# Two chained transformer blocks on one core: the modulation product half a quarter sooner in the first MLP, its column sums as rows in four groups of 32 output partitions, then turned

## Chip, cores and metric

One Trainium2 chip, one NeuronCore. The metric is device time in microseconds of one execution, the median of several runs. All inputs and outputs are float32.

## What is computed

A 512-token sequence of width 1024 goes through a first block (mixer of convolution and retention, then a squared-ReLU MLP, then a norm) and a second block (adaptive norm, two kinds of attention, squared-ReLU MLP). What matters here is the first MLP and the modulation vector that the second block needs:

```python
def sq_relu_mlp(u, w_up, w_down):
    hdn = jax.nn.relu(u @ w_up)          # w_up 1024 x 4096
    return (hdn * hdn) @ w_down          # w_down 4096 x 1024
...
ada = (c @ w_ada + b_ada)                # c 1 x 1024, w_ada 1024 x 6144
shift1, scale1, gate1, shift2, scale2, gate2 = jnp.split(ada, 6, axis=-1)
h = rmsnorm(x, g_norm1) * (1.0 + scale1) + shift1
```

## The kernel before, in words

Activations lie feature-major: `xres[P, KC, T]` holds 8 chunks of 128 features by 512 tokens. Every large product is made of **units**: one 1024x128 weight block against all 8 chunks of the input, giving 128 output features by 512 tokens in one PSUM bank. Float32 precision comes from three reduced-precision products per chunk, high x high, high x low, low x high, so a unit is 24 matmuls of 512 columns (`unit`, L539 to L555). `two_units` runs two units alternately, chunk by chunk.

The weights of a unit pass through four slots (slot s = unit number mod 4): SyncE issues the load into `raw` (L338) once GpSimd has freed the slot, ScalarE casts it to the high half `w_hi` (L1045), GpSimd subtracts for the low half `w_lo` (L511), TensorE then uses both. ScalarE casts two units ahead (`ahead`), in its program order just before it reads the result of the current unit.

The first MLP goes through four quarters q. A quarter is 8 up units (hidden features) and 8 down units. In this document U0 to U7 are the up units and D0 to D7 the down units of a quarter, of the first quarter where nothing else is said; O0 to O7 are the units of the output projection before it. U0 and U1, and U4 and U5, are run as pairs by `two_units`; the others singly. After each up unit ScalarE makes the ReLU (L1238) and its square, rounded (L1240), VectorE the exact square (L1830) and the low half (L1835); after each down unit VectorE scales (L1852) and adds to `xres` (L1856). D0's and D4's chunks wait for the low halves one by one (`mlp_h`).

The modulation product c @ w_ada is made on VectorE beside this. `w_ada` (24 MB) comes in 32 **pieces** of 128 rows by 1536 columns, 768 KB each, into two buffers `adaw[:, b, :]`. `ada_piece` (L1793 to L1805) multiplies a piece by 128 entries of c and adds it to `acc[128, 6144]`. Pieces stand at every odd unit, U1, U3, U5, U7, D1, D3, D5, D7, with b = 0, 1, 0, 1, and so on; the load of a piece (L420) stands on SyncE's queue right behind the weight load of that unit and waits for `ada_used`, that is for VectorE to be done with the piece that had the same buffer. SyncE, ScalarE, GpSimd, VectorE and TensorE all run their own instructions strictly in the order written here by hand.

What is left is the sum of `acc` over its 128 partitions. TensorE makes it as 48 products `ada_columns` (L777): 128 columns of `acc` as weights, one column of ones as input, one column of output. In the last down units (`with_columns`) a group of two columns follows each of chunks 2 to 7 of D4, D5 and D7; the last twelve come after `both_sums` (the sums for the next norm) and `roots_turned` (its roots, turned into rows). `modulation(0)` (L1807) reads the first half and makes the gains before D7's result, `modulation(1)` the second half after the norm.

Of the kernel before, what the change touches and what calls it, by code (L numbers as in the profile page):

```python
# [27 lines left out]
ALU = mybir.AluOpType  # L28
# [54 lines left out]
MLPS = ["mlp", "mlp2"]  # L83

# [85 lines left out]
def build(nc, tab, x, norm1_g, w_in, conv_w, conv_norm_g, ret_norm_g, w_out, norm2_g, w_up, w_down,  # L170
# [29 lines left out]
    with ctx:  # L200
# [67 lines left out]
        gones = sb("gones", [P, 2], where=one)  # L268
# [60 lines left out]
        def _(sp):  # L329
# [66 lines left out]
            with sp.Fori(0, KC // 4) as i:  # L396
                for s in range(4):
                    load(st_out, s, i, (whole, cols(w_out, i * 4 * P + s * P)))

            def mlp(st, up, down, with_ada):  # L400
                with sp.Fori(0, NF) as q:
                    for d in range(2):
                        with sp.Fori(0, 2) as i:
                            for s in range(4):
                                if d == 0:
                                    src = cols(up, q * D + i * 4 * P + s * P)
                                else:
                                    src = down.rearrange("(q k p) n -> q p k n", q=NF, p=P)[
                                        ds(q, 1), :, :, ds(i * 4 * P + s * P, P)
                                    ].rearrange("q p k n -> p (q k) n")  # L410
                                load(st, s, q * 4 + 2 * d + i, (whole, src))
                                if with_ada and s % 2:
                                    b = s // 2


                                    sp.wait_ge(sem(f"ada_used{b}"), q * 4 + 2 * d + i + 1)
                                    sp.wait_ge(sem("mix_done"), 1)
                                    src = w_ada_2.rearrange("(q k p) n -> q k p n", q=NF, p=P)[
                                        ds(q, 1), d, :, ds(i * 3 * D + b * 3 * D // 2, 3 * D // 2)]
                                    sp.dma_start(adaw[:, b, :], src.rearrange("q p n -> p (q n)")  # L420
                                                 ).then_inc(sem(f"ada_in{b}"), 16)

            mlp(st_mlp, w_up, w_down, True)
# [8 lines left out]
            sp.wait_ge(sem("ada_sum"), 2)  # L432
# [29 lines left out]
            sp.wait_ge(sem("ada_ready"), 2)  # L462
# [74 lines left out]
        def _(pe):  # L537
# [83 lines left out]
            def bias_rows_made():  # L621

                pe.wait_ge(sem("bias_in"), 32)
                pe.matmul(ps[0:HEADS, SB, :], rbias[:], oneh[:, 0:T], start=True, stop=True)
                pe.matmul(ps[0:HEADS, OU, 0:P], rbias[:], oneh[:, T:NREL], start=True, stop=True
                          ).then_inc(sem("brow_done"), 1)

                pe.wait_ge(sem("vrow_in"), 16 * (len(VECS) - 1))
                pe.transpose(ps[:, OU, P:P + NVEC], vrow[:], ident[0:NVEC, 0:NVEC]).then_inc(sem("vec_turned"), 1)
# [145 lines left out]
            def ada_columns(m0, m1, done=False):  # L775
                for m in range(m0, m1):
                    last = pe.matmul(ps[:, (SB, OU)[m // (3 * KC)], m:m + 1], acc[:, m * P:(m + 1) * P], ones[:, 0:1],  # L777
                                     start=True, stop=True)
                if done:
                    last.then_inc(sem("ada_sum"), 1)  # L780

            def with_columns(s, m0, done):


                pe.wait_ge(sem("acc_done"), 2 * (NF * 4 - 1) + m0 // 12)
                for k in range(KC):
                    unit(st_mlp, s, NF * 4 - 1, y_hi, y_lo, part=(k, k + 1), opens=(k == 0), closes=(k == KC - 1))
                    if k >= 2:
                        ada_columns(m0 + 2 * (k - 2), m0 + 2 * (k - 1), done and k == KC - 1)
# [15 lines left out]
            pe.wait_ge(sem("ada_ready"), 2)  # L805
# [231 lines left out]
        def _(act):  # L1037
# [33 lines left out]

            def norm(name, shift):
                if name == "n3":
# [3 lines left out]
                    act.activation(rinv[:, NT:2 * NT], mneg[:, NT:2 * NT], ACT.Sqrt).then_inc(sem("norm_root"), 1)  # L1077
                else:
# [61 lines left out]
            act.wait_ge(sem("vec_turned"), 1)  # L1140
# [87 lines left out]
            def mlp(st, name, next_norm):  # L1228
# [18 lines left out]
                def down(q, i, last=False):  # L1247
                    for s in range(4):
                        if not (last and st is st_mlp2 and s + AHEAD >= 4):
                            ahead(st, s, q * 4 + 2 + i)  # L1250
                        if last is not False and st is st_mlp:
                            m = i * 4 + s
                            square(next_norm, m, "mlp_x", mlp_before(name) + (NF - 1) * KC)
# [275 lines left out]
        def _(dve):  # L1529
# [246 lines left out]

            def wout(st, scale, done, next_norm, gained=False):
                clear_total(next_norm)
                for i in range(KC // 4):
                    for s in range(4):  # L1780
# [7 lines left out]
                        if i * 4 + s < KC - 1:  # L1788
                            add_square(next_norm, i * 4 + s)

            wout(st_out, lambda m: 1.0, "x_mixed", "n2", gained=True)


            def ada_piece(q, d, i, b):
                n = q * 4 + 2 * d + i
                dve.wait_ge(sem(f"ada_in{b}"), 16 * (n + 1))
                dve.wait_ge(sem("acc_done"), 2 * n + b + 1)
                a = acc[:, ds(i * 3 * D + b * 3 * D // 2, 3 * D // 2)]
                c = vec[:, ds(VAT["c_2"] + 2 * q + d, 1)]
                if isinstance(q, int) and q == 0 and d == 0:  # L1800
                    dve.tensor_scalar(a, adaw[:, b, :], c, None, ALU.mult).then_inc(sem("acc_done"), 1)
                else:
                    dve.scalar_tensor_tensor(a, adaw[:, b, :], c, a, ALU.mult, ALU.add).then_inc(sem("acc_done"), 1)  # L1803
                dve.wait_ge(sem("acc_done"), 2 * n + b + 2)
                dve.sem_inc(sem(f"ada_used{b}"), 1)  # L1805

            def modulation(half):  # L1807

                a, c = half * 3 * KC, slice(half * 3 * KC, (half + 1) * 3 * KC)
                gain, g_at = (gain1, VAT["g_norm1_2"]) if half == 0 else (gain2, VAT["g_norm2_2"])  # L1810
                dve.wait_ge(sem("ada_sum"), half + 1)
                dve.tensor_tensor(ada[:, c], ps[:, (SB, OU)[half], c], vec[:, VAT["b_ada_2"] + a:VAT["b_ada_2"] + a + 3 * KC],
                                  ALU.add).then_inc(sem("ada_ready"), 1)
                dve.wait_ge(sem("ada_ready"), half + 1)
                dve.scalar_tensor_tensor(gain[:], ada[:, a + KC:a + 2 * KC], 1.0, vec[:, g_at:g_at + KC],
# [6 lines left out]
            def mlp(st, name, scale, with_ada, next_norm, factor=None):  # L1822
                def up(q):
                    with dve.Fori(0, 2) as i:
                        for s in range(4):
                            if factor is not None and s == 0:
                                wait(dve, sem("mlp_x"), q * KC + mlp_before(name))

                            dve.wait_ge(bank_free[s], st.turn(s, q * 4 + i) + 1)
                            dve.tensor_tensor(nt[:, s % 2, :], nsq[:, s % 2, :], nsq[:, s % 2, :], ALU.mult  # L1830
                                              ).then_inc(sem("mlp_sq"), 1)
                            dve.wait_ge(sem("mlp_sq"), q * KC + i * 4 + (mlp_before(name) + s + 1))
                            dve.wait_ge(sem("mlp_hi"), q * KC + i * 4 + (mlp_before(name) + s + 1))
                            m = ds(i * 4 + s, 1)
                            dve.tensor_tensor(y_lo[:, m, :], nt[:, s % 2:s % 2 + 1, :], y_hi[:, m, :], ALU.subtract  # L1835
                                              ).then_inc(sem("mlp_h"), 1)
                            dve.wait_ge(sem("mlp_h"), q * KC + i * 4 + (mlp_before(name) + s + 1))
                            if with_ada and s % 2:
                                ada_piece(q, 0, i, s // 2)

                def down(q, i, last=False):
                    for s in range(4):
                        final = with_ada and last and i == 1 and s == 3
                        if with_ada and s % 2 and not final:
                            ada_piece(q, 1, i, s // 2)
                        n, m = q * KC + i * 4 + (mlp_before(name) + s), i * 4 + s
                        if factor is None:
                            add(st, q * 4 + 2 + i, s, n, m, scale(m), "mlp_x")
                        else:
                            dve.wait_ge(used[s], st.turn(s, q * 4 + 2 + i) + 1)  # L1850
                            wait(dve, sem("mlp_x"), n)
                            dve.tensor_tensor(nt[:, 0, :], ps[:, s, :], factor[:], ALU.mult  # L1852
# [373 lines left out]
```

## Time and profile before

| | us |
|---|---|
| median of 3 runs | 1390.85 (1390.78 to 1392.7) |
| the profiled execution's own time | 1392.73 |
| its span, first to last instruction | 1390.9 |
| TensorE busy | 1364.6 (98%) |
| VectorE / ScalarE / GpSimd busy | 818.7 / 517.0 / 561.8 |
| mean granted clock of TensorE, share of full speed | 0.994 |
| output projection O3 to O7, and first MLP | about 221 to 609 |
| sums, roots and columns, to the next projection's first matmul | 609 to 618 |

The profile gives for each engine its instructions with start and length. Line numbers are those of the kernel before. "Idle before <-X" names the instruction whose signal ended the engine's wait. Lengths of matmuls overlap: of a stream of them the distance between starts is what counts.

### The profile page before, as it was taken

Reading aid. Unit: us, or ns where it says so; the run is one execution under the profiler, and the core shown is the slowest. Engines: PE = TensorE matmul, PEld = TensorE weight load, DVE = VectorE, ACT = ScalarE, POOL = GpSimd, SP = SyncE. Lnnn points to the kernel's source line nnn. Section 1 sums busy time; section 2 is a strip of 40 time slices with the busy share of each in tenths; the row PEclk is TensorE's granted clock in tenths of the full one; section 3 lists DMA queues with packets and bytes.
Section 4 is the critical chain, followed back from the end, with each engine's and each line's share of the span. In section 5 each row is a group of like instructions: output and inputs, shape, how many; then the busy total and the mean of one; then the engine's idle time right before and its main releaser. Section 6 shows DMA issues by size and latency. Waiting matters only on the chain.

```text
span 1390.9 us, 18371 instructions
## 1 busy us (share of the span) xinstructions
PE 1364.6 (98%) x6358; PEld 1104.4 (79%) x6358; DVE 818.7 (59%) x1074; ACT 517.0 (37%) x794; POOL 561.8 (40%) x230
## 2 busy tenths in 40 slices
PE   7999999999999999999999999999999999999997
PEld 6777787888888888887777777888878888888886
DVE  4455577574765746885988866334554343352474
ACT  4333224331422314234356665322345323142233
POOL 3334245353553545424322223443525535345361
PEclk9999999999999999989999999999999999999999
DMA  7643234366383763623522232333422423323221
GB/s 206 143 84 91 77 106 140 86 191 173 111 236 96 219 184 106 197 55 106 77 73 60 82 92 79 104 91 92 138 74 91 132 80 108 89 88 118 81 91 61
DMA packets 216323, 156.66 MB, mean 113 GB/s; under 512 B 8996, under 2 KB 197792, under 8 KB 216136
## 3 DMA queue, kind: packets, MB, share of 16 engines
q1 hardware_dynamic: 215800, 154.62, 39.8%
q10 hardware_dynamic: 464, 1.27, 0.3%
q8 instruction: 36, 0.59, 0.2%
q14 instruction: 23, 0.19, 0.0%
HBM read 151.13 MB, written 4.74 MB: 112 GB/s over the span
## 4 chain that ended last, share of the span: by engine, by line
PE 50%; DVE 2%; ACT 1%; issue 0%; POOL 0%; ACTq 0%; DVEq 0%
PE ps L551 28%; PE ps L998 12%; PE ps L947 3%; PE ps L886 2%; PE ps L863 1%; PE ps L850 1%; PE ps L836 1%; PE ps L837 1%; DVE work L2069 1%; DVE work L2066 0%; PE ps L840 0%; DVE work L2051 0%; DVE top L2049 0%; DVE sel L2054 0%; POOL w_lo L511 0%
## 5 line engine op out<-in xcount | busy, mean ns | idle before, releaser
L511 POOL TENSOR_TENSOR w_lo<-raw,w_hi 128x1024 fp32r<-128x1024 f32 x222 | 558.4, 2524 | 795.1 <-ACT w_hi L1045 790.3
L551 PE MATMUL ps<-u_hi,w_hi 128*128 128x512 f32 x1016 | 411.4, 405 | 6.8 <-POOL w_lo L511 2.3
L551 PE MATMUL ps<-u_hi,w_lo 128*128 128x512 f32 x1016 | 398.5, 392 | 0.0
L551 PE MATMUL ps<-u_lo,w_hi 128*128 128x512 f32 x1016 | 398.3, 392 | 0.0
L1045 ACT ACTIVATE w_hi<-raw 128x1024 fp32r<-128x1024 f32 x221 | 231.3, 1053 | 247.8 <-PE ps L998 91.0
L551 PEld LDWEIGHTS ps<-u_hi,w_hi 128*128 128x128 f32 x1016 | 193.3, 190 | 48.9 <-issue 5.4
L551 PEld LDWEIGHTS ps<-u_hi,w_lo 128*128 128x128 f32 x1016 | 192.1, 189 | 41.2
L551 PEld LDWEIGHTS ps<-u_lo,w_hi 128*128 128x128 f32 x1016 | 192.8, 190 | 39.2 <-issue 1.9
L551 PE MATMUL ps<-y_hi,w_hi 128*128 128x512 f32 x320 | 126.7, 396 | 0.1
L551 PE MATMUL ps<-y_lo,w_hi 128*128 128x512 f32 x320 | 124.6, 389 | 0.0
L551 PE MATMUL ps<-y_hi,w_lo 128*128 128x512 f32 x320 | 124.6, 389 | 0.0
L1238 ACT ACTIVATE nsq<-ps 128x512 f32<-128x512 f32 x64 | 38.0, 593 | 214.4 <-PE ps L551 214.3
L998 PE MATMUL ps<-w_hi,y_hi 128*128 128x512 f32 x256 | 99.6, 389 | 0.0
L998 PE MATMUL ps<-w_lo,y_hi 128*128 128x512 f32 x256 | 99.6, 389 | 0.0
L998 PE MATMUL ps<-w_hi,y_lo 128*128 128x512 f32 x256 | 99.6, 389 | 0.0
L1830 DVE TENSOR_TENSOR nt<-nsq 128x512 f32<-128x512 f32 x32 | 46.3, 1446 | 62.9 <-ACT nsq L1238 60.9
L1901 DVE TENSOR_TENSOR nt<-nsq 128x512 f32<-128x512 f32 x32 | 38.6, 1207 | 75.1 <-ACT nsq L1238 74.1
L1803 DVE SCALAR_TENSOR_TENSOR acc<-adaw,vec,acc 128x1536 f32 (+1 forms) x28 | 73.8, 2637 | 4.3 <-DVE y_lo L1835 4.0
L551 PEld LDWEIGHTS ps<-y_hi,w_hi 128*128 128x128 f32 x320 | 60.1, 188 | 12.9 <-issue 0.6
L551 PEld LDWEIGHTS ps<-y_hi,w_lo 128*128 128x128 f32 x320 | 60.1, 188 | 12.7
L1923 DVE SCALAR_TENSOR_TENSOR nt<-ps,rinv,gate_row 128x512 f32<-128x512 f32 x21 | 15.8, 751 | 91.6 <-PE ps L998 91.6
L551 PEld LDWEIGHTS ps<-y_lo,w_hi 128*128 128x128 f32 x320 | 60.1, 188 | 12.0 <-issue 0.2
(268 smaller groups left out, 1771.9 us busy)
## 6 DMA issues: line engine op xcount, KB each, us to landing
raw<-w_in SPq DMA_DIRECT2D x69, 512.0 KB, 3.8
raw<-w_mlp SPq DMA_DIRECT2D x64, 512.0 KB, 3.8
adaw<-w_ada SPq DMA_DIRECT2D x32, 768.0 KB, 4.6
raw<-w_up SPq DMA_DIRECT2D x32, 512.0 KB, 6.2
raw<-w_down SPq DMA_DIRECT2D x32, 512.0 KB, 6.5
raw<-w_out SPq DMA_DIRECT2D x16, 512.0 KB, 4.0
bias_rows<-fbrow SPq DMA_DIRECT2D x4, 640.0 KB
xtok<-x SPq DMA_DIRECT2D x4, 512.0 KB, 6.4
```

The source lines that it names most:

```text
L511: pool.tensor_tensor(w_lo[:, s, :], raw[:, s, :], w_hi[:, s, :], ALU.subtract).then_inc(lo_ready[s], 1)
L551: last = pe.matmul(ps[0:cols, bank, :], w[:, s, c], r[:, k, :], start=(k == ks[0] and w is w_hi and r is r_hi), stop=(k == ks[-1] and w is ...
L836: pe.matmul(ps[:, bank, 0:keys], q_up[:, at, q], k_both[:, at, 0:keys], start=True, stop=False)
L886: last = pe.matmul(ps[:, i, :], u[:, k, t], w[:, s, c], start=(k == 0 and u is u_hi and w is w_hi), stop=(k == KC - 1 and u is u_lo))
L947: last = pe.matmul(ps[:, b, :], w[:, 2, c], r[:, k, :], start=(k == k0 and w is w_hi and r is y_hi), stop=(k == k0 + NQ - 1 and w is w_lo))
L998: last = pe.matmul(ps[:, i, :], h[:, k, t], w[:, s, c], start=(k == 0 and h is y_hi and w is w_hi), stop=(k == KC - 1 and h is y_lo))
L1045: act.activation(w_hi[:, s, :], raw[:, s, :], ACT.Copy).then_inc(hi_ready[s], 1)
L1238: act.activation(nsq[:, s % 2, :], ps[:, s, :], ACT.Relu).then_inc(bank_free[s], 1)
L1803: dve.scalar_tensor_tensor(a, adaw[:, b, :], c, a, ALU.mult, ALU.add).then_inc(sem("acc_done"), 1)
L1830: dve.tensor_tensor(nt[:, s % 2, :], nsq[:, s % 2, :], nsq[:, s % 2, :], ALU.mult).then_inc(sem("mlp_sq"), 1)
L1901: dve.tensor_tensor(nt[:, s % 2, :], nsq[:, s % 2, :], nsq[:, s % 2, :], ALU.mult).then_inc(sem("mlp_sq"), 1)
L1923: dve.scalar_tensor_tensor(gated[i], ps[:, i, :], facts[:, i:i + 1], gate_row[:, c], ALU.mult, ALU.mult).then_inc(bank_free[i], 1)
```

## The change

Three things. (1) The order of the pieces: the first two move to O4 and O6 in the output projection, six to U1, U2, U3, U5, U6, U7 of the first quarter, and from D1 on each piece stands half a quarter sooner than before; the last quarter's down half has none. The wait for `mix_done` moves from each piece to one place ahead of O5's load. (2) The sum over partitions: for each 512 columns of `acc` one product with 32 columns of `pick` as weights (one column of ones, the rest zeros), written to output partitions 32g to 32g + 31 of one bank, g = 0 to 3. Four such products (`ada_rows(0, 0)`) go ahead of D4, eight between `both_sums` and `roots_turned`. (3) ScalarE copies that bank to SBUF (`ada_row_copy`), TensorE turns it in four blocks (`ada_turned`), between D5 and D6 and behind `roots_turned`, and `modulation` reads the turned layout.

```diff
+FIRST_PIECES = [(0, 1, 0), (0, 1, 1), (1, 0, 0), (1, 0, 1), (1, 1, 0), (1, 1, 1)]
+PIECES = 8 * NF
...
+            def ada_load(q, d, i, b):
+                sp.wait_ge(sem(f"ada_used{b}"), q * 4 + 2 * d + i + 1)
...
+                sp.dma_start(adaw[:, b, :], src.rearrange("q p n -> p (q n)")).then_inc(sem(f"ada_in{b}"), 16)
+            for i in range(KC // 4):
                 for s in range(4):
                     load(st_out, s, i, (whole, cols(w_out, i * 4 * P + s * P)))
+                    if i == 1 and s == 0:
+                        sp.wait_ge(sem("mix_done"), 1)
+                    if i == 1 and s % 2 == 0:
+                        ada_load(0, 0, 0, s // 2)
...
+            def down_loads(q, with_ada):
+                with sp.Fori(0, 2) as i:
+                    for s in range(4):
+                        down_load(q, i, s)
+                        if with_ada and s % 2:
+                            ada_load(q + 1, 0, i, s // 2)
+
+            for i in range(2):
+                for s in range(4):
+                    up_load(0, i, s)
+                    if s > 0:
+                        ada_load(0, *FIRST_PIECES[3 * i + s - 1])
+            down_loads(0, True)
...
-            def ada_columns(m0, m1, done=False):
-                for m in range(m0, m1):
-                    last = pe.matmul(ps[:, (SB, OU)[m // (3 * KC)], m:m + 1], acc[:, m * P:(m + 1) * P], ones[:, 0:1],
-                                     start=True, stop=True)
+            def ada_rows(n, at, opens=True, closes=True):
+                for g in range(4):
+                    j = 4 * n + g
+                    last = pe.matmul(ps[32 * g:32 * g + 32, SB, :], pick[:, 32 - at:64 - at], acc[:, j * QW:(j + 1) * QW],
+                                     start=opens, stop=closes)
...
-            with_columns(0, 0, False)
-            with_columns(1, 12, True)
-            unit(st_mlp, 2, NF * 4 - 1, y_hi, y_lo)
-            with_columns(3, 24, False)
+            def ada_turned(half):
+                pe.wait_ge(sem("arow_ready"), half + 1)
+                for b in range(4):
+                    last = pe.transpose(ps[:, OU, b * P:(b + 1) * P], adaw[:, half, b * P:(b + 1) * P], ident)
+                last.then_inc(sem("ada_sum"), 1)
+
+            pe.wait_ge(sem("acc_done"), PIECES + 1)
+            pe.wait_ge(sem("squares"), 7)
+            ada_rows(0, 0)
+            for s in range(2):
+                unit(st_mlp, s, NF * 4 - 1, y_hi, y_lo)
+            ada_turned(0)
+            for s in range(2, 4):
+                unit(st_mlp, s, NF * 4 - 1, y_hi, y_lo)
 
             both_sums()
-            pe.wait_ge(sem("acc_done"), 2 * NF * 4 + 1)
-            ada_columns(36, 42)
+            ada_rows(1, 0, closes=False)
+            ada_rows(2, 1, opens=False)
             roots_turned()
-            ada_columns(42, 48, True)
+            pe.wait_ge(sem("ada_ready"), 1)
+            ada_turned(1)
...
+            def ada_row_copy(half):
+                act.wait_ge(sem("ada_sum"), 2 * half + 1)
+                act.activation(adaw[:, half, 0:QW], ps[:, SB, :], ACT.Copy).then_inc(sem("arow_ready"), 1)
...
+                        if gained and i == 1 and s % 2 == 0:
+                            ada_piece(0, 0, 0, s // 2)
...
+                for i in range(2):
+                    for s in range(4):
+                        up_step(0, i, s)
+                        if s > 0:
+                            ada_piece(0, *FIRST_PIECES[3 * i + s - 1])
```

## Rows read from the trace of the kernel before

**Rows 1.** The profile page, busy time by engine.
```profile
PE 1364.6 (98%) x6358; PEld 1104.4 (79%) x6358; DVE 818.7 (59%) x1074; ACT 517.0 (37%) x794; POOL 561.8 (40%) x230
```

**Rows 2.** The waits by releaser, TensorE, 261 to 612 us: total, times, longest.
```profile
PE ps L551 <- POOL w_lo L511: 1.4, 3, 0.5
```

**Rows 3.** The waits by releaser, SyncE's DMA queue, 195 to 620 us.
```profile
SPq L420 <- DVEq L1805: 275.9, 30, 23.9
```

**Rows 4.** The timeline of SyncE's queue, 195 to 345 us: start, length, instruction, count.
```profile
241.42 3.13 SPq L338 DMA_DIRECT2D raw<-w_up  x2
268.83 0.35 SPq L420 DMA_DIRECT2D adaw<-w_ada  x1
269.41 1.00 SPq L338 DMA_DIRECT2D raw<-w_up  x2
```

**Rows 5.** The timeline of ScalarE, 205 to 345 us, idle time and its releaser in brackets.
```profile
272.39 0.60 ACT L1238 ACTIVATE nsq<-ps 128x512 f32<-128x512 f32 x1 [3.06 <-PE ps L551]
...
275.39 1.06 ACT L1045 ACTIVATE w_hi<-raw 128x1024 fp32r<-128x1024 f32 x1 [1.64 <-DMA raw<-w_up]
...
294.15 0.60 ACT L1238 ACTIVATE nsq<-ps 128x512 f32<-128x512 f32 x1 [3.07 <-PE ps L551]
...
299.02 1.06 ACT L1045 ACTIVATE w_hi<-raw 128x1024 fp32r<-128x1024 f32 x1 [3.51 <-DMA raw<-w_down]
...
300.93 1.06 ACT L1045 ACTIVATE w_hi<-raw 128x1024 fp32r<-128x1024 f32 x1 [0.84 <-DMA raw<-w_down]
```

**Rows 6.** The timeline of VectorE, 205 to 345 us.
```profile
217.96 0.69 DVE L1748 TENSOR_TENSOR y_lo<-nt,y_hi 128x512 fp32r<-128x512 f32 x1 [0.70 <-ACT y_hi L1194]
...
262.14 2.19 DVE L1830 TENSOR_TENSOR nt<-nsq 128x512 f32<-128x512 f32 x1 [0.87 <-ACT nsq L1238]
...
264.50 2.63 DVE L1835 TENSOR_TENSOR y_lo<-nt,y_hi 128x512 f32 x1 [0.17 <-DVE nt L1830]
...
267.50 1.02 DVE L1801 TENSOR_SCALAR acc<-adaw,vec 128x1536 f32 x1 [0.38 <-DVE y_lo L1835]
...
291.04 1.02 DVE L1801 TENSOR_SCALAR acc<-adaw,vec 128x1536 f32 x1 [0.37 <-DVE y_lo L1835]
```

**Rows 7.** The timeline of GpSimd, 195 to 345 us.
```profile
261.37 5.21 POOL L511 TENSOR_TENSOR w_lo<-raw,w_hi 128x1024 fp32r<-128x1024 f32 x2 [6.07 <-ACT w_hi L1045]
...
276.52 2.39 POOL L511 TENSOR_TENSOR w_lo<-raw,w_hi 128x1024 fp32r<-128x1024 f32 x1 [4.74 <-ACT w_hi L1045]
```

**Rows 8.** The timeline of TensorE's weight loads in D7, 596 to 609.5 us.
```profile
603.13 0.64 PEld L777 LDWEIGHTS ps<-ones,acc 128*128 128x128 f32 x4
...
604.27 0.64 PEld L777 LDWEIGHTS ps<-ones,acc 128*128 128x128 f32 x4
```

**Rows 9.** The timeline of TensorE, 255 to 262.5 us: a plain float32 product, 512 columns.
```profile
260.32 1.02 PE L565 MATMUL ps<-nsq,ones 128*128 128x512 f32 x2
```

**Rows 10.** The timeline of TensorE, 733 to 745 us: 64 output partitions each.
```profile
734.06 0.27 PE L863 MATMUL ps<-probt_even,vtoks 128*64 128x128 f32 x1
734.07 0.27 PE L863 MATMUL ps<-probt_odd,vtoks 128*64 128x128 f32 x1
734.17 0.27 PE L863 MATMUL ps<-probt_even,vtoks 128*64 128x128 f32 x1
```

**Rows 11.** The timeline of all engines, 600 to 650 us, from D6's end on.
```profile
606.66 2.13 DVE L1815 SCALAR_TENSOR_TENSOR gain<-ada,vec 128x8 f32<-128x8 f32 x1
...
609.31 0.69 DVE L1852 TENSOR_TENSOR nt<-ps,nrs 128x512 f32<-128x512 f32 x1 [0.32 <-PE ps L551]
...
612.52 1.73 PE L777 MATMUL ps<-ones,acc 128*128 128x1 f32 x12
...
616.85 0.75 DVE L1575 SCALAR_TENSOR_TENSOR u_lo<-nt,ada,u_hi 128x512 fp32r<-128x512 f32 x1
...
618.27 0.77 PE L551 MATMUL ps<-u_hi,w_hi 128*128 128x512 f32 x1
```

**Rows 12.** Busy time by stretch: length, PE, PEld, DVE, ACT, POOL, granted clock, DMA.
```profile
620.00:622.00 2.00, 2.00 (x6) 1.52 (x6) 2.00 (x4) 1.07 (x2) 0.00 (x0) 0.50 0.94 340
```

More of the change, by code:

```diff
@@ L267, in build @@
         adaw = sb("adaw", [P, 2, 6 * D // 4], where=one)
-        gones = sb("gones", [P, 2], where=one)
+        gones, pick = sb("gones", [P, 2], where=one), sb("pick", [P, 64], where=one)
         one.close()
@@ L397, in _ @@
                 for s in range(4):
                     load(st_out, s, i, (whole, cols(w_out, i * 4 * P + s * P)))
[L400 to L421, printed above, removed]
@@ L425, in _, with quarter @@
+            def quarter(q, with_ada):
+                with sp.Fori(0, 2) as i:
+                    for s in range(4):
+                        up_load(q, i, s)
+                        if s % 2:
+                            ada_load(q, 1, i, s // 2)
+                down_loads(q, with_ada)
+            with sp.Fori(1, NF - 1) as q:
+                quarter(q, True)
+            quarter(NF - 1, False)
             load(st_idx, 0, 0, (whole, cols(w_in_2, W2_QI)))
@@ L1814, in modulation @@
-                dve.wait_ge(sem("ada_ready"), half + 1)
-                dve.scalar_tensor_tensor(gain[:], ada[:, a + KC:a + 2 * KC], 1.0, vec[:, g_at:g_at + KC],
+                dve.wait_ge(sem("ada_sum"), 2 * half + 2)
+                turned_ada = ps[:, OU, :].rearrange("p (b g r) -> p g b r", b=4, g=4)
+                for n in range(1 + half):
+                    c = slice(a + 16 * n, a + 16 * (n + 1))
+                    dve.tensor_tensor(ada[:, c].rearrange("p (g b) -> p g b", g=4), turned_ada[:, :, :, n],
+                                      vec[:, VAT["b_ada_2"]:VAT["b_ada_2"] + 6 * KC][:, c].rearrange("p (g b) -> p g b", g=4),
+                                      ALU.add).then_inc(sem("ada_ready"), 1)
@@ L1816, in modulation @@
+                dve.wait_ge(sem("ada_ready"), 1 + 2 * half)
+                at = KC + half * 3 * KC
+                dve.scalar_tensor_tensor(gain[:], ada[:, at:at + KC], 1.0, vec[:, g_at:g_at + KC],
                                          ALU.add, ALU.mult).then_inc(sem("gains"), 1)
@@ L1825, in up @@
                         for s in range(4):
[L1826 to L1839, printed above, removed]
+                            up_step(q, i, s)
@@ L1862, in down @@
-                        if last and i * 4 + s < KC - 1:
-                            add_square(next_norm, i * 4 + s)
-                        if with_ada and last and i == 1 and s == 2:
-                            modulation(0)
-                        if final:
-                            ada_piece(q, 1, i, s // 2)
-                if factor is None:
-                    first = 0
-                else:
-                    first = 1
-                    up(0)
-                    dve.wait_ge(sem("norm_sum"), NORMS.index({"mlp": "n2", "mlp2": "n4"}[name]))
-                    dve.tensor_scalar(factor[:], ps[:, SA, :], 1.0 / D, EPS, ALU.mult, ALU.add
-                                      ).then_inc(sem("mean_sq"), 1)
-                    dve.wait_ge(sem("mean_sq"), MLPS.index(name) + 1)
-                    dve.reciprocal(factor[:], factor[:]).then_inc(sem("factor"), 1)
-                    dve.wait_ge(sem("factor"), MLPS.index(name) + 1)
-                    for i in range(2):
-                        down(0, i)
@@ L1883, in mlp @@
-                with dve.Fori(first, NF - 1) as q:
+                        dve.wait_ge(used[s], st.turn(s, q * 4 + 2 + i) + 1)
+                        wait(dve, sem("mlp_x"), n)
+                        dve.tensor_tensor(nt[:, 0, :], ps[:, s, :], factor[:], ALU.mult
+                                          ).then_inc(bank_free[s], 1)
+                        dve.wait_ge(bank_free[s], st.turn(s, q * 4 + 2 + i) + 1)
+                        dve.tensor_tensor(xres[:, ds(m, 1), :], nt[:, 0:1, :], xres[:, ds(m, 1), :], ALU.add
+                                          ).then_inc(sem("mlp_x"), 1)
@@ new lines, in down @@
+                        if last and m < KC - 1:
+                            add_square(next_norm, m)
+                        if last and m == KC - 2:
+                            modulation(0)
+                for i in range(2):
+                    for s in range(4):
+                        up_step(0, i, s)
+                        if s > 0:
+                            ada_piece(0, *FIRST_PIECES[3 * i + s - 1])
+                dve.wait_ge(sem("norm_sum"), NORMS.index("n2"))
+                dve.tensor_scalar(factor[:], ps[:, SA, :], 1.0 / D, EPS, ALU.mult, ALU.add
+                                  ).then_inc(sem("mean_sq"), 1)
@@ L1884, in mlp @@
+                dve.wait_ge(sem("mean_sq"), MLPS.index(name) + 1)
+                dve.reciprocal(factor[:], factor[:]).then_inc(sem("factor"), 1)
+                dve.wait_ge(sem("factor"), MLPS.index(name) + 1)
+                for i in range(2):
+                    down(0, i)
+                with dve.Fori(1, NF - 1) as q:
                     up(q)
```

102 lines of the change are left out of this document (51 added, 51 removed).

## The prediction

> **What bounds the kernel now.** I read the page first: TensorE is busy for 1364.6 of 1390.9 us [rows 1], so only what makes TensorE wait or work counts. Next the waits by releaser, over the first MLP: TensorE waits for split weights three times, 1.4 us in all [rows 2]. There is no slack left to win there, only some to lose. Then the waits of SyncE's DMA queue: from 195 to 620 us it stands for 275.9 us at the modulation load (L420), until VectorE has used up the piece before in that buffer [rows 3]. The queue is strictly in order, so every weight load written behind a modulation load leaves no sooner than that piece is used. Today this harms nothing, because the two buffers alternate every second unit and each is reused after four units. The timelines of the first quarter show by how much: the weights of U4 and U5 are issued at 241.4 us, 31 us before TensorE wants them, and the queue then stands until VectorE's U1 piece ends (267.50 + 1.02 = 268.5) [rows 4, 6].
>
> **Part 1: two pieces in the out projection.** VectorE gets two steps of 1.0 us [rows 6] and SyncE waits for mix_done (VectorE's last conv step ends at 218.65, same group) before it issues the load that follows O4's. The cover is that O5 to O7 are two and more units of 5.44 us ahead, while load, cast and split take 10 us after mix_done; TensorE stands at O2 then. If that cover were gone each load would cost up to 4 us. The loads of U2 and U3 now wait for the pieces of O4 and O6, some 13 us later than before, yet still reach ScalarE as it wants them. I cost this at nothing.
>
> **Part 2: six pieces in eight units.** In U0 to U7 the pieces stand at U1, U2, U3, U5, U6, U7, buffers 0, 1, 0, 1, 0, 1. So U3's load waits for U1's piece, and U4's weights stand behind it; U7's load waits for U5's piece, and D0's weights stand behind that. The distance of four units has become two. With rows of before:
> (a) U1's piece ends at 268.5 today, because its subtraction is held to 267.1 by GpSimd's pair of splits (261.4 to 266.6) [rows 6, 7]. The second of those, U4's, will not be there yet, so I take 267.1. Issue of the modulation load and the weights behind it takes 0.9 us [rows 4]: 268.0. Such a load landed 6.0 us after issue (269.41 to 275.39) [rows 4, 5]: 274.0. Cast 1.06, split 2.4 [rows 5, 7]: 277.5. U4 is due when U3 ends, 272.3 [rows 5]. U4 and U5 alternate chunk by chunk, so after one chunk of 0.68 us TensorE needs U5's weights too. The second load lands 1.9 us after the first (299.02, 300.93) [rows 5], ScalarE puts U2's ReLU and square between the casts, and GpSimd and VectorE take turns: 280.4 against 273.0. **Loss 7.4.**
> (b) U2's ReLU now waits behind the late cast (275.1), its two VectorE steps are each held by a split, its piece ends at 282.3. U6's weights leave at 282.9 and are ready 9.5 us later, 292.4; U5 ends 280.4 + 15 x 0.68 = 290.6. **Loss 1.8.**
> (c) From U5's end (272.3 + 10.9 = 283.2) to its piece's end (292.06) it took 8.9 us [rows 6]; the piece becomes a multiply-add, 0.8 us longer. 290.6 + 9.7 = 300.3, D0's weights leave at 301.2 and are ready at 310.7. U7 ends at 292.4 + 10.9 = 303.3. **Loss 7.4.**
> (d) U6's ReLU stands behind D0's cast on ScalarE (308.3). VectorE then has four steps and U6's piece, three of them held by the splits of D0 and D1; U7's low half comes at 318.0, while D0's last chunk is due at 315.5. **Loss 2.5.**
> (e) D2's weights wait for U6's piece (316.1) and are ready at 326.2; D1 ends at 324.2. **Loss 2.0.** Behind D3 the distance is four units again.
> Sum 21.1. Below, if GpSimd never held VectorE (each step 0.69), the same working gives 4.7 + 5.3 + 1.0 = 11. Above, each of the two long stops brings TensorE's clock down: the next paragraphs price it. I take 21, because the held steps stand in the rows.
>
> **Part 3: the last down half.** Removed: 36 single-column products in D4, D5 and D7, in groups of two. With a group between them, chunks start 1.14 us apart (603.13, 604.27) [rows 8] instead of 0.68, so 0.46 a group: 6 groups a unit, 5.5 in D4 and D5, 2.8 in D7. U4 to U7 took 294.15 - 272.39 = 21.76, or 5.44 a unit [rows 5]. Added before D4: four float32 products of 512 columns. One such product, two instructions, spans 1.02 us with its drain [rows 9], 0.86 in a row (an estimate from that and the 0.17 of drain). Two products with 64 output partitions start 0.01 apart and the pair repeats every 0.11 [rows 10], so two run side by side. I take four side by side for 32 partitions, 0.9 and 0.3 for changing shape; one after another it would be 3.4. ScalarE's copy lies beside D4; four turns of 128 columns are 0.5. Net for D4 to D6: 5.5 - 1.7 = 3.8.
> The Trainium skill, TensorE: Matmul & The Clock Gate, Part 3, states a speedup of 2.38 for three such column tiles. No row here has four; by that figure the twelve products would take some 4.3 us and not 2.6, and the sum would be 1.7 higher.
> D7 gives back less than its 2.8, since VectorE is late next: between D6's result and D7's it makes the sums and the first gains, of which one step is held for 2.13 us by a split [rows 11]. Today D7's long unit hides that (VectorE even waits 0.32 us, to 609.31 [rows 11]). Without the columns I have VectorE ready 6.4 us after D6's end and TensorE after 5.4: gain 2.8 - 1.0 = 1.8.
>
> **Part 4: between D7 and the index projection.** The eight row products (1.7 us) replace twelve columns (1.73) [rows 11] ahead of the roots' turn: even. The other twelve go from behind it. TensorE began the next unit at 618.27, though its first input was ready at 616.85 + 0.75 = 617.6 [rows 11]: gain 0.6. The copy on ScalarE (0.6) runs beside the root's turn. Clock: at 620 us the granted clock is 0.50, the lower level of 1.2 GHz, six products in 2 us [rows 12], after a stretch of one-column products; with the full clock the 5.7 us until it came back would have been 3.0. If the wider products keep the clock, 2.7 more is gained; since TensorE now also idles about 1 us there, I take none.
> Tail: 3.8 + 1.8 + 0.6 = 6.2, between 3 (VectorE fully late, turns at double price) and 9.
>
> **Sum.** The profiled execution took 1392.7 (span 1390.9). 1392.7 + 21.1 - 6.2 = 1407.6; it stood 1.9 above the median of the runs, so for them 1405.8, say 1406.
>
> **Rivals.**
> *The loads arrive in time* (other side). Place: the queue at U3's modulation load. It decides if U1's piece ended by 262: 272.3 less 3.5 for cast and split, 6.0 for landing, 0.9 for issue. U1's ReLU itself only ends at 262, and the piece today at 268.5. Even if a load alone in the queue landed in 4 us, some stop stays. Were it so, only the tail counts: 1390.9 - 6.2 = 1384.7. Chance 0.08.
> *Only the first stop.* VectorE catches up during it, and (b) to (e) vanish: 1390.9 + 7.4 - 6.2 = 1392. Against it: D0's load hangs on U5's piece, which follows U5's end whatever went before. Chance 0.08.
> *Row products one after another*: 12 x 0.86 is 10.3 instead of 2.6, and the roots' turn waits: 1414. The pairs in rows 10 speak against it. Chance 0.08.
> *The clock falls at each long stop*: twice 2.7 from rows 12, partly inside later waits: 1408 to 1411. Chance 0.2. [...]
> The forecast itself 0.56. That the product isn't finished before D4 is excluded: its last piece now stands at U7 of the fourth quarter.
>
> **Numbers.** 1406 is the forecast's. The range 1394 to 1415 takes in losses of 11 to 26 against gains of 3 to 9. Faster by over 0.2% (about what a measurement here can tell from no change) 0.09, within 0.2% 0.06 (only the first stop), slower 0.85.
>
> **What would show it.** In the profile after: TensorE waiting for w_lo (L511) at the first chunk of U4, U5 and D0, 5 us and more, and for y_lo at D0's last chunk; SyncE at the modulation load until about 267 and 300 us, with ScalarE's cast waiting for DMA behind; D4 to D7 at 5.44 us each; groups of four row products 0.9 us long. It is wrong if no wait of TensorE over 2 us stands between 261 and 330 us, or if SyncE issues U4's weights before 262 us.

## The result, and the profile after

The changed kernel takes 1403.43 us (median of 4 runs, 1402.91 to 1405.74), the kernel before on the same chip 1391.16 (4 runs, 1390.78 to 1392.7): a ratio of 1.0093, 95% interval 1.008 to 1.0105, or 12.3 us slower. The forecast was 1406, in a range of 1394 to 1415.

The page of the changed kernel, busy time by engine:

```profile
PE 1357.6 (97%) x6290; PEld 1092.5 (78%) x6294; DVE 814.0 (58%) x1078; ACT 517.8 (37%) x796; POOL 564.7 (40%) x230
```

TensorE has 68 matmul records fewer than in [rows 1] and works 7.0 us less, in a span 10.2 longer (1401.1): it works less and waits 17 us more. The waits by releaser, 195 to 640 us (total, times, longest), the largest of TensorE and the largest of SyncE's queue:

```profile
PE ps L574 <- POOL w_lo L534: 15.2, 7, 6.5
```
```profile
SPq L404 <- DVEq L1823: 274.2, 30, 20.5
```

The 1.4 us of [rows 2] have become 15.2. The queue stands at the modulation load (now L404) as long as before [rows 3], so the total of that wait says nothing about the change; what has changed is which loads stand behind it. The timeline of TensorE in the first quarter, all its idle times over 0.9 us in brackets:

```profile
274.65 0.79 PE L574 MATMUL ps<-u_hi,w_hi 128*128 128x512 f32 x1 [3.93 <-POOL w_lo L534]
...
277.41 0.80 PE L574 MATMUL ps<-u_hi,w_hi 128*128 128x512 f32 x1 [1.12 <-POOL w_lo L534]
...
306.71 0.77 PE L574 MATMUL ps<-y_hi,w_hi 128*128 128x512 f32 x1 [6.47 <-POOL w_lo L534]
...
321.83 0.50 PE L574 MATMUL ps<-y_hi,w_hi 128*128 128x512 f32 x1 [1.82 <-POOL w_lo L534]
```

These are U4's first chunk, U5's first, D0's first and D2's first: 13.3 us of stops. What released them is read backwards through the other engines: GpSimd (the splits of U4, U5 and of D0, D1), ScalarE (the casts before them), SyncE's queue and VectorE (U1's steps and piece, then U5's piece). In the rows, first the queue, then GpSimd, ScalarE and VectorE:

```profile
264.64 0.34 SPq L404 DMA_DIRECT2D adaw<-w_ada  x1
265.07 1.01 SPq L341 DMA_DIRECT2D raw<-w_up  x2
...
296.72 0.34 SPq L404 DMA_DIRECT2D adaw<-w_ada  x1
297.45 1.01 SPq L341 DMA_DIRECT2D raw<-w_down  x2
```
```profile
272.24 5.12 POOL L534 TENSOR_TENSOR w_lo<-raw,w_hi 128x1024 fp32r<-128x1024 f32 x2 [10.02 <-ACT w_hi L1073]
...
304.12 5.13 POOL L534 TENSOR_TENSOR w_lo<-raw,w_hi 128x1024 fp32r<-128x1024 f32 x2 [10.62 <-ACT w_hi L1073]
```
```profile
257.43 0.60 ACT L1271 ACTIVATE nsq<-ps 128x512 f32<-128x512 f32 x1 [4.43 <-PE ps L574]
...
271.11 1.06 ACT L1073 ACTIVATE w_hi<-raw 128x1024 fp32r<-128x1024 f32 x1 [9.85 <-DMA raw<-w_up]
...
302.99 1.06 ACT L1073 ACTIVATE w_hi<-raw 128x1024 fp32r<-128x1024 f32 x1 [10.73 <-DMA raw<-w_down]
```
```profile
260.59 2.18 DVE L1870 TENSOR_TENSOR nt<-nsq 128x512 f32<-128x512 f32 x1 [1.00 <-ACT nsq L1271]
...
263.53 1.02 DVE L1819 TENSOR_SCALAR acc<-adaw,vec 128x1536 f32<-128x1536 f32 x1
...
294.81 1.82 DVE L1821 SCALAR_TENSOR_TENSOR acc<-adaw,vec,acc 128x1536 f32<-128x1536 f32 x1
```

U1's piece ends at 264.55, the load behind it leaves at 264.64 and U4's at 265.07; ScalarE has them 6.0 us later, after waiting 9.85 us for them. U5's piece ends at 296.63, the queue goes on at 296.72, and ScalarE gets D0's weights 5.5 us after their issue. Before, U4's weights left at 241.4 [rows 4]. The granted clock, by stretch (us, TensorE busy, instructions, granted clock, DMA share, GB/s):

```profile
274.00:278.00 4.00, 2.23 (x4) 0.50 0.00 0
278.00:282.00 4.00, 4.00 (x14) 0.68 0.48 129
305.00:310.00 5.00, 3.29 (x8) 0.50 0.01 3
310.00:315.00 5.00, 5.00 (x21) 0.88 0.42 114
...
629.00:632.00 3.00, 2.05 (x10) 1.00 0.61 160
```

After each long stop (the one at U4 and U5, and the one at D0) TensorE works at the lower level, 1.2 GHz, for some microseconds; a product then starts 0.43 us after the one before it, at the full level 0.23 (a chunk of three in 0.68):

```profile
278.43 0.63 PE L574 MATMUL ps<-u_hi,w_lo 128*128 128x512 f32 x1
278.86 0.63 PE L574 MATMUL ps<-u_hi,w_hi 128*128 128x512 f32 x1
```

Last the tail, TensorE from D3's end to the index projection:

```profile
596.90 1.06 PE L802 MATMUL ps<-acc,pick 128*32 128x512 f32 x8
...
624.00 2.44 PE L802 MATMUL ps<-acc,pick 128*32 128x512 f32 x16
...
629.95 0.47 PE L574 MATMUL ps<-u_hi,w_hi 128*128 128x512 f32 x1 [0.95 <-DVE u_lo L1610]
...
641.82 0.47 PE L574 MATMUL ps<-u_hi,w_hi 128*128 128x512 f32 x1 [0.71 <-issue]
```

Four row products of 512 columns take 1.06 us from the start of the first to the end of the last; D4 to D7 have nothing between their chunks. The last row is the third unit of the index projection: no product starts for 1.10 us ahead of it, where the kernel before goes on without a break. What holds TensorE there the profile does not show.

**A ledger.** The profiled executions differ by up to 3.6 us in when U0 ends, in either direction, also between kernels that have the same code up to there. So the parts are counted from U0's ReLU (258.98 us before; 257.43 after, in the rows above). D4 is VectorE's first step on the first quarter's D4 (before 321.27, after 338.50), "norm" its first step of norm n3's products, "idx" TensorE's first product of the turn by w_in behind the index projection, whose distance to the span's end is the same in both to 0.13 us.

| us | ReLU to D4 | D4 to norm | norm to idx | sum |
|---|---|---|---|---|
| before | 62.29 | 294.05 | 24.79 | 381.13 |
| after | 81.07 | 289.02 | 22.66 | 392.75 |
| difference | +18.8 | -5.0 | -2.1 | +11.6 |

Of the 18.8, 13.3 are the stops. By the distances between starts, some 4.2 more are the products at the lower clock (2.1 behind each of the two stops), and about 1 is what the four stops cost beside their idle time, where the stream of products breaks off and begins again. The second column is -6.9 from the last quarter's D4 to D7, +0.5 spread over the quarters before, +0.8 because TensorE waits for VectorE's work on D7's result (0.91 us of idle time ahead of the sums at L603), and +0.6 mostly because the eight row products take 2.44 where the twelve columns took 1.73 [rows 11]. Of the last column, -0.5 is the projection's start, nearer to norm than before, -2.5 is its clock (the row of 629 to 632 us, against [rows 12]), and +0.9 is the pause at 641.82.

### The profile page after: what moved, and what is told of

It is laid out like the page before. It is cut to its first block, busy times and chain, and to the rows that moved or that the text cites. A ratio compares the mean times of both kernels' runs of the same rounds, so it can differ in the third digit from the quotient of the medians.

```text
span 1401.1 us, 18109 instructions
## 1 busy us (share of the span) xinstructions
PE 1357.6 (97%) x6290; PEld 1092.5 (78%) x6294; DVE 814.0 (58%) x1078; ACT 517.8 (37%) x796; POOL 564.7 (40%) x230
## 4 chain that ended last, share of the span: by engine, by line
PE 50%; DVE 2%; ACT 1%; issue 0%; POOL 0%; ACTq 0%; DVEq 0%
PE ps L574 28%; PE ps L1026 12%; PE ps L975 3%; PE ps L914 2%; PE ps L891 1%; PE ps L878 1%; PE ps L864 1%; PE ps L865 1%; DVE work L2104 1%; DVE work L2101 0%; DVE work L2086 0%; PE ps L868 0%; DVE top L2084 0%; DVE sel L2089 0%; POOL w_lo L534 0%
## 5 line engine op out<-in xcount | busy, mean ns | idle before, releaser
L1821 DVE SCALAR_TENSOR_TENSOR acc<-adaw,vec,acc 128x1536 f32 (+1 forms) x28 | 67.4, 2407 | 4.8 <-DVE y_lo L1875 4.3
```

## The experiments

All ratios are against the kernel before, measured on the same chip at the same time, with their 95% interval. Three chips were used, one for the first four experiments, one for the next three and one for the last two; the kernel before takes 1391.17, 1391.08 and 1391.46 us on them. "Shift" is the change of the ledger's first column against before.

**Weights ahead of the piece loads**, in the first quarter alone; nothing but SyncE's order is touched:

```diff
 up_load(0, 0, 3)
-ada_load U3; up_load(0, 1, 0); up_load(0, 1, 1)
+up_load(0, 1, 0); up_load(0, 1, 1); ada_load U3
 ...
+(the same for U6, U7 ahead of U5's piece, D0, D1 ahead of U7's)
```

> Changed kernel, but on SyncE's queue the weights of U4 and U5 are issued ahead of U3's modulation load, those of U6 and U7 ahead of U5's, those of D0 and D1 ahead of U7's. The pieces themselves stay where the change puts them, on VectorE too. Theory (the order on the queue is the whole loss): TensorE's waits for w_lo between 261 and 330 us fall from 13.3 us to under 1, the shift of 18.8 us at the end of the first quarter is gone, and the time is 1403.4 - 18.8 = 1384.6, 6.5 below the kernel before. Rival (the extra pieces load VectorE or the DMA rings too much in the first quarter, whatever the order): waits of TensorE of several us stay, for y_lo or w_lo, and the time is 1393 or more.

Measured 1388.56 (11 runs), ratio 0.9984 [0.9975, 0.9993]; shift +5.0. Both long stops are gone and 14.9 of the change's time is back: the cause of the loss is the order in one queue. It is not the full gain expected, since one stop remains. SyncE's queue, then TensorE at D2:

```profile
289.21 5.73 SPq L404 DMA_DIRECT2D adaw<-w_ada  x2
295.04 1.00 SPq L341 DMA_DIRECT2D raw<-w_down  x2
```
```profile
304.62 0.50 PE L593 MATMUL ps<-y_hi,w_hi 128*128 128x512 f32 x1 [2.05 <-POOL w_lo L553]
```

D2's weights still stand behind the load that waits for U6's piece (until 294.5), and TensorE waits for them; y_lo costs 0.7 more. The other 1.7 of the shift of 5.0 is the clock, which falls behind D2's stop. The four experiments below that have the same order in this quarter stop there for 1.9 to 2.1 us too, but in the profiled execution of three of them (the old columns, the one group, the rows split) the clock does not fall, and the shift is 3.3 or 3.4; in the fourth (the gains) it falls and the shift is 5.0. So 1.7 us of a difference between two of these kernels can be the clock of one execution.

**Only the first hold removed:** U3's piece load alone moved behind U4's and U5's weights.

```diff
-ada_load U3; up_load(0, 1, 0); up_load(0, 1, 1)
+up_load(0, 1, 0); up_load(0, 1, 1); ada_load U3
```

> Changed kernel, but only U3's modulation load is put behind the weights of U4 and U5; U7's stays ahead of D0's weights. Theory (each of the two places stops TensorE by itself): the first stop and its slow clock, 7.6 us, are gone, D0's stop of 6.5 us, the slow clock after it and D2's stay: 1403.4 - 7.6 = 1395.8. Rival (the first stop makes the engines late and so causes the second): D0's stop is gone as well, 1385.

Measured 1395.65 (7 runs), ratio 1.0034 [1.0023, 1.0045]; shift +11.3. TensorE at D0:

```profile
297.03 0.77 PE L584 MATMUL ps<-y_hi,w_hi 128*128 128x512 f32 x1 [6.57 <-POOL w_lo L544]
```

D0's stop is as long as in the changed kernel (6.47). The two long stops are independent, each with its own piece load, and the rival "only the first stop" is false from this side too.

**TensorE kept at work during the stops.** Ahead of U4 six and ahead of D0 ten float32 products of 384 columns into a bank that nobody reads; this adds work to the computation and leaves its results as they are.

```diff
+keep_warm(6)
 mlp_up(st_mlp, "n2", 0, 1)
+keep_warm(10)
```

> Changed kernel, and TensorE fills most of the two stops with float32 products of 384 columns into an unused bank: 6 ahead of U4, 10 ahead of D0 (extra work, no result of it is used). Theory A (the loads set when TensorE goes on, and the slow clock of some 5 us after the stops is absorbed by the next wait): the granted clock stays 1.00 at 274 to 281 and 306 to 311 us, but U6 and D2 wait longer for their weights instead; the time moves by less than 1.5 us: 1402 to 1403.5. Theory B (the slow clock is paid in full): 5 us faster, 1398.5.

Measured 1404.54 (4 runs), ratio 1.0104 [1.0089, 1.0119]; shift +19.6. TensorE:

```profile
268.69 4.03 PE L791 MATMUL ps<-small,ones 128*128 128x384 f32 x12
272.75 0.50 PE L574 MATMUL ps<-u_hi,w_hi 128*128 128x512 f32 x1
...
275.51 0.50 PE L574 MATMUL ps<-u_hi,w_hi 128*128 128x512 f32 x1 [1.80 <-POOL w_lo L534]
...
310.73 0.50 PE L574 MATMUL ps<-y_hi,w_hi 128*128 128x512 f32 x1 [1.23 <-DVE y_lo L1881]
...
319.30 0.79 PE L574 MATMUL ps<-y_hi,w_hi 128*128 128x512 f32 x1 [2.16 <-POOL w_lo L534]
```
```profile
274.00:278.00 4.00, 2.49 (x11) 1.00 0.00 0
...
305.00:310.00 5.00, 4.50 (x20) 1.00 0.00 0
```

From U0's ReLU (255.56 here) U4 starts at 17.2 and U5 at 19.95; in the changed kernel at 17.2 and 19.98. The clock stays at the full 2.4 GHz behind both stops, and the time is no shorter. What TensorE gains by the clock it mostly loses again: U6 waits 1.0 for its weights (287.02), D0's last chunk 1.2 for y_lo, D2 2.2. At D2's first product, 63.7 us behind U0's ReLU against 64.4 in the changed kernel, 0.7 of the 4.2 us is left; the other 3.5 lay inside waits that would otherwise have been there. Even the 0.7 is then gone, because here the clock falls behind D2's stop (0.57 over 319 to 323 us), which in the changed kernel it does not. So the unchanged total is in part this second fall; what shows that loads and low halves set when TensorE may go on is the place of D2.

**The old columns on the new loads** (the first experiment, with the column sums and their reading as before; the pieces stay where the change put them):

```diff
-ada_rows(...), ada_row_copy(...), ada_turned(...)
+ada_columns(...) between the chunks of D4, D5, D7 and behind the roots' turn
```

> x1_weights_first with the partition sums as in the kernel before (48 one-column products, in D4, D5, D7 and around the roots' turn), the pieces staying early. What it differs from x1 by is the worth of the row products. By the shifts in the trace that is 7.1 in D4 to D7, less 0.9 for VectorE being late, less 0.2 at the roots, plus 1.6 from the clock that does not fall: 7.6. So 1384.6 + 7.6 = 1392. Rival (the gain of the tail comes from the pieces leaving the last down half, not from the row products): 1386 or less.

Measured 1395.92 (6 runs), ratio 1.0036 [1.0024, 1.0049], 7.4 above the first experiment. Its norm comes 294.31 us behind D4 and idx 24.64 behind that, as before the change (294.05, 24.79); the first experiment has 289.34 and 22.65. The row products are worth 7.4 us by the medians and 7.0 by these two columns, which leave the first quarter out.

**All four row products into one group of output partitions**, on top of the first experiment. This kernel leaves out keeping the four parts of the modulation apart: it adds them up in one row, so its result is not the reference's, and only its time is of use.

```diff
-ps[32 * g:32 * g + 32, SB, :] ... start=opens, stop=closes
+ps[0:32, SB, :] ... start=opens and g == 0, stop=closes and g == 3
```

> x1_weights_first, but the four row products of a group all go to output partitions 0 to 31, so that they cannot run side by side; the modulation is then wrong (sums of four parts in one row). Theory (four groups of 32 output partitions run side by side): the four ahead of D4 take 3.4 us instead of 0.9, the eight behind D7 6.8 instead of 2.2 and hold the roots' turn: 7 us slower than x1, 1391.6. Rival (they run one after another in the changed kernel too): no difference.

Measured 1397.06 (6 runs), ratio 1.0036 [1.0024, 1.0047], 8.5 above the first experiment. TensorE, and below it the eight of the first experiment:

```profile
583.02 3.62 PE L821 MATMUL ps<-acc,pick 128*32 128x512 f32 x8
...
612.67 8.75 PE L821 MATMUL ps<-acc,pick 128*32 128x512 f32 x16
```
```profile
608.35 2.78 PE L821 MATMUL ps<-acc,pick 128*32 128x512 f32 x16
```

Four products take 3.62 instead of 1.06, eight 8.75 instead of 2.78 (both eights in part at the lower clock). That is 8.5, the whole difference: with four groups of 32 output partitions the products do run side by side, and without that the new form is no faster than the old columns (1.0036 for both).

**The first gains behind D7's result** (first experiment, and VectorE makes the first gains after D7's addition instead of ahead of it):

```diff
-if last and m == KC - 2:
+if last and m == KC - 1:
     modulation(0)
```

> x1_weights_first, with modulation(0) on VectorE behind D7's addition instead of ahead of it. Theory (one of its steps is held 2.15 us by GpSimd's split and makes VectorE 0.9 us late for D7's result): D7's scaling begins as TensorE ends, 0.9 us faster than x1: 1383.7. Rival (VectorE is not on the path there, or the gains are then late for the norm): same as x1 or slower.

Measured 1386.78 (6 runs), ratio 0.9967 [0.9955, 0.9979]: 1.8 below the first experiment, with intervals that just touch, and norm is 1.5 nearer to D4 (287.88). Only 0.4 of that is the gains: VectorE takes up D7's result 281.95 us behind D4 instead of 282.36. The other 1.05 comes behind D7's sums, where in the first experiment the clock fell and the eight row products took 2.78, while here it stayed and they took 1.92. In the changed kernel the gains hold VectorE ahead of D7's result like this:

```profile
618.62 2.15 DVE L1858 SCALAR_TENSOR_TENSOR gain<-ada,vec 128x8 f32<-128x8 f32 x1
620.80 0.17 DVE L1862 TENSOR_TENSOR gain<-gain,vec 128x8 f32<-128x8 f32 x1
620.89 0.69 DVE L1893 TENSOR_TENSOR nt<-ps,nrs 128x512 f32<-128x512 f32 x1
```

An instruction on 8 columns takes 2.15 us while GpSimd subtracts (618.14 to 620.75), and 0.17 where it does not. It ends at 620.77; TensorE was done with D7 at 620.43, and VectorE takes up its result at 620.89.

**The second row products split** (on the last one: four of the eight behind the roots' turn, their turn behind two units of the index projection, and ScalarE's copy of the bank between chunks of the norm):

```diff
-ada_rows(2, 1); roots_turned(); ada_turned(1); two_units(...)
+roots_turned(); ada_rows(2, 1); two_units(...); ada_turned(1)
```

> x6_gains_late, with the last four row products behind the roots' turn instead of ahead of it, ScalarE's copy of the bank behind the fourth chunk of the norm and the turn of the second half after the first two index units. Theory (eight row products, 2.2 us, hold the roots' turn 0.95 us, and TensorE idles 0.95 us later anyway): 0.5 us faster than x6, 1383.2. Rival (the copy holds ScalarE's chunks, or the turn costs more where nothing hides it): same or up to 1 us slower.

Measured 1388.17 (11 runs), ratio 0.9978 [0.9969, 0.9987]; no gain. Norm to idx is 24.18 instead of 22.65. The turn itself costs next to nothing, as it stands where the other kernels have their pause ahead of the third unit. What is new is a stop at the turn by w_in. TensorE, then SyncE's queue:

```profile
632.53 0.50 PE L933 MATMUL ps<-w_hi,u_hi 128*128 128x512 f32 x1 [1.14 <-POOL w_lo L553]
```
```profile
625.34 0.88 SPq L341 DMA_DIRECT2D raw<-w_in  x2
```

The next loads stand on SyncE's queue behind a wait for that turn (`ada_sum`), and leave at 625.34; in the gains' experiment they leave at 613.54. It is the queue's order again.

**D2's weights ahead too** (on the gains' experiment: D2's weights ahead of U7's piece load, D3's ahead of D1's):

```diff
+down_load(0, 0, 2)
 ada_load U7
-ada_load D1
-down_load(0, 0, 2)
 down_load(0, 0, 3)
+ada_load D1
```

> x6_gains_late, and on SyncE's queue the weights of D2 also go ahead of U7's modulation load and those of D3 ahead of D1's. In x1 to x7 D2's weights still waited for U6's piece: a stop of 2 us at D2's first chunk with a slow clock behind it. Theory (what is left of x1's loss is that one place of the queue): the stop at D2 is gone, the first quarter's shift against the kernel before falls from 3.3 to 5 us to 1 or less, and the time is 1386.8 - 3 = 1383.8. Rival (VectorE, with six pieces in eight units, is late by itself): the shift stays at 3 or more and the time at 1386 to 1387.

Measured 1384.77 (6 runs), ratio 0.9955 [0.9943, 0.9967]: 6.7 us faster than the kernel before, and the lowest median of all. Shift +1.0; D2's stop is gone and only y_lo's 0.7 is left, with the break in the stream.

**Distance four again.** The gains late, SyncE's order the plain one, and the pieces every second unit throughout (O4, O6, U1, U3, ..., the last two in D1 and D3 of the last quarter), so that each buffer is reused after four units:

```diff
-pe.wait_ge(sem("acc_done"), PIECES + 1)
+pe.wait_ge(sem("acc_done"), PIECES - 1)
 ...
 ada_rows(0, 0)
 ...
+pe.wait_ge(sem("acc_done"), PIECES + 1)
 ada_rows(1, 0, closes=False)
```

> x6_gains_late with the pieces at O4, O6 and then at every odd unit as in the kernel before, loads right behind the weights of that unit: no buffer is reused in fewer than four units. The last two pieces (columns from 3072 on) stand at D1 and D3 of the last quarter, where only the rows behind D7 need them. Theory (the distance of two is what stopped TensorE, and with four the simple order of the queue does no harm): no stop over 1 us in the first quarter, shift there 0 to 0.5, tail 8.6 shorter than before by the shifts of x6: 1391.1 - 8.4 = 1382.7. Rival (the first two pieces in the output projection cost something themselves): a shift of 1 us or more stands already at U0's first ReLU to U7, and the time is 1385 or more.

Measured 1386.19 (6 runs), ratio 0.9966 [0.9955, 0.9978]. The shift is 0.0 (62.28 against 62.29). Busy time of 261 to 345 us, and SyncE's queue:

```profile
261.00:345.00 84.00, 84.00 (x372) 69.56 (x371) 52.62 (x40) 22.86 (x28) 41.44 (x16) 1.00 0.63 175
```
```profile
249.78 0.34 SPq L408 DMA_DIRECT2D adaw<-w_ada  x1
250.21 1.01 SPq L345 DMA_DIRECT2D raw<-w_up  x2
...
274.09 0.34 SPq L408 DMA_DIRECT2D adaw<-w_ada  x1
274.52 1.01 SPq L345 DMA_DIRECT2D raw<-w_down  x2
```

TensorE works all 84 us. U4's weights leave 15 us earlier than in the changed kernel and D0's 23, with piece loads ahead of them as there: a hold does no harm at this distance. Of the 3.5 by which it misses 1382.7, 2.5 are in the tail: norm comes 290.35 behind D4 instead of 287.88. TensorE ends D7 0.8 sooner than in the gains' experiment, but 1.9 are lost because VectorE is behind, and 1.4 to the clock. VectorE's addition of D7's result (and those of D5's and D6's before it) is held by GpSimd's split; in the gains' experiment the same addition takes 0.69:

```profile
602.01 2.12 DVE L1892 TENSOR_TENSOR xres<-nt,xres 128x512 f32<-128x512 f32 x1
```

The eight row products of this run, and of the gains' experiment, on TensorE:

```profile
605.83 3.50 PE L797 MATMUL ps<-acc,pick 128*32 128x512 f32 x16
```
```profile
609.80 1.92 PE L821 MATMUL ps<-acc,pick 128*32 128x512 f32 x16
```

and the granted clock beside them, again first this run, then the gains' experiment:

```profile
606.00:608.00 2.00, 2.00 (x12) 0.51 0.03 8
```
```profile
609.00:611.00 2.00, 2.00 (x20) 1.00 0.03 8
```

The same eight products take 1.92 at 2.4 GHz and 3.50 at 1.2. The experiment before this one has the low clock too, and for longer (3.64 for the eight, norm at 290.54, of which the clock is the whole 2.7). Both stretches follow the one-column sums of norm n3. What decides whether the clock falls there was not settled. It need not be the kernel: the six executions of the experiment before this one go from 1382.06 us at a mean clock of 0.999 to 1386.78 at 0.996.

## Why the prediction was right, point by point

**The direction and the mechanism held.** It named the queue's order, the two pieces, the three engines behind them and the three units that would wait; the reordered queue alone takes back 14.9 us, and distance four the whole shift. Medians moved by 12.3 where 15.2 was forecast (1406 less 1390.85).

**Part 1, nothing:** right. TensorE is busy 54.68 us of 195 to 250 in both traces.

- **(a) 7.4:** close. U5's first product comes 6.2 late, of which 3.93 + 1.12 are stops. U1's piece ended 7.1 us after U0's ReLU; from 267.1 the forecast had it at 8.1. The queue, 6.0 for landing, cast and split came as taken.
- **(b) 1.8:** no wait in the changed kernel. TensorE at the low clock was itself 1.5 later by U6; with the clock kept, the wait appears at 1.0.
- **(c) 7.4:** 6.6, of which 6.47 is the stop. Only one of U5's two steps was held by a split, and U5 ended less late.
- **(d) 2.5:** the step that failed, in its mechanism. No wait at D0's last chunk, because TensorE went through D0 at the low clock: U7's low half was there at 313.2. With the clock kept the wait is 1.2. What stands in its place is 2.2 of low clock and broken stream behind D0's stop.
- **(e) 2.0:** 1.82.

The sum, 21.1, measured 18.8. The forecast took no low clock, and the rival that did (the clock falls at each long stop) added twice 2.7 to it. The clock did fall, and cost twice 2.1, but for the most part not in addition: it stands in the place of (b) and (d), as the run with dummy products shows. The rival had the event right and the price wrong. The forecast had (a), (c) and (e) right as mechanisms; that (b) and (d), together 4.3, come near the 3.7 that the low clock and the broken stream cost in their place is luck.

**The tail, 6.2:** 7.1 in the ledger's last two columns, 7.4 by the medians of an experiment. The total is near, but misses of its terms cancel. D4 to D7 gave back 6.9; the forecast had 3.8 + 2.8. VectorE late for D7 was taken at 1.0 and is 0.4 late; 0.8 stands there, because TensorE, without its last columns, reaches the wait sooner. The group of four was taken at 0.9 and spans 1.06, the eight at 1.7 and take 2.44, in part at the lower clock; that delays norm by 0.6, where the forecast had them even. The 0.6 expected at the index projection came as 0.5. The clock, taken at nothing there, gave 2.5: TensorE starts the projection at full clock, which in [rows 12] it had not. The pause of 0.9 ahead of the third unit, which the forecast did not have, took part of that back.

**Row products one after another:** false, by 8.5 us. The Trainium skill, TensorE: Matmul & The Clock Gate, Part 3, states a speedup of 2.38 for three column tiles. Here four tiles of 32 partitions give 3.62 / 1.06 = 3.4; no run has three. All twelve products take 1.06 + 2.44 = 3.5 us, between the 2.6 of the forecast and the 4.3 that it worked out from that 2.38, with the clock down in part of the eight; at the full clock, in the gains' experiment, they take 3.0.

**Loads in time:** false, by 13.3 us of stops.

## What to carry to other kernels

In an in-order DMA queue a load that waits for a buffer holds every load behind it, so the figure to check when work is moved is the distance at which a buffer is reused against the lead of the loads behind it: four units cost nothing here, two cost 18.8 us. Either restore the distance or put the loads that the bottleneck needs ahead of the load that waits; such moves, with the gains' steps of VectorE put later (0.4 us), turned a change 0.9% slower into one 0.45% faster. And when waits are priced, a slow clock behind a stop is no separate cost if what comes next waits for loads anyway: add only what would still be there at full clock.

## What the runs showed of the hardware, not expected

- Four float32 products of 512 columns into four groups of 32 output partitions take 1.06 us, into one group 3.62.
- VectorE on 128 x 8 values takes 0.17 us alone and 2.15 while GpSimd subtracts, and then ends within 0.02 us of GpSimd's instruction: in these rows the length goes by the neighbour's instruction, not by the size of VectorE's own. The step just ahead of it, 128 x 16 and read from PSUM, took 0.17 under the same subtraction.
- The granted clock behind the one-column sums of norm n3 differs between profiled executions with the same instructions there: 1.00 in the gains' experiment, about 0.50 for 3 to 6 us in others, worth 1.0 to 2.7 us. In the kernel before, too, it falls there (0.81 over 613 to 614 us, 0.50 from 614 on), though TensorE was busy for 4.94 of the 5 us from 609 to 614.
